# Peer expert retrieval in a two-layer trunk: the U dot products read the normed tokens from SBUF instead of from a copy in PSUM

## What is computed

```
def peer(h, wq, sub_keys, peer_u, peer_v):
    ...
    def block(xb):                       # 128 tokens
        ...                              # scores, three top-16, giving idx
        idx = jnp.take_along_axis(cidx, pos, axis=-1)      # (128, 8 heads, 16)
        g = jax.nn.softmax(sc, axis=-1)
        act = jax.nn.gelu(jnp.einsum('nd,nhkd->nhk', xb, peer_u[idx]), approximate=False)
        w = (g * act).astype(xb.dtype)
        return jnp.einsum('nhk,nhkd->nd', w, peer_v[idx])
```

## Time and profile before

| what | value |
| --- | --- |
| median of 3 runs | 4716.82 us (4715.45 to 4723.3) |
| the profiled execution's own time | 4724.11 us |
| its span, first to last instruction | 4722.3 us |
| PE busy | 3807.0 us, 81% |
| DVE busy | 2801.9 us, 59% |
| POOL busy | 2699.4 us, 57% |
| ACT busy | 1047.4 us, 22% |
| DMA packets of the POOL queue | 1342.34 MB of 1454.78 MB |

### The profile page before, as it was taken

The page is one execution under the profiler, slowest core; times in us unless marked ns, Lnnn a source line. Parts: engine busy times, 40 slices in busy tenths (PEclk is TensorE's granted clock), DMA queues, the critical chain, the costliest instruction groups (busy, mean ns, idle before and its releaser), DMA issues.

```text
span 4722.3 us, 40282 instructions
## 1 busy us (share of the span) xinstructions
PE 3807.0 (81%) x11914; PEld 1770.3 (37%) x11914; DVE 2801.9 (59%) x6305; ACT 1047.4 (22%) x2385; POOL 2699.4 (57%) x2759
## 2 busy tenths in 40 slices
PE   6999776888888888888778997688878878878877
PEld 3466532333333333333224575333333333333332
DVE  1612547666666667667634455576676776666763
ACT  1122211222222222222212141122222222222221
POOL 1800006667667667667755500277777777777775
PEclk8999588999999999999998995899999999999999
DMA  5112139999999999999981101399999999999998
GB/s 182 37 55 81 39 121 358 398 404 403 398 394 404 396 394 400 399 398 403 403 351 51 33 24 69 110 410 409 409 405 406 404 406 406 405 404 405 402 407 341
DMA packets 512186, 1454.78 MB, mean 308 GB/s; under 512 B 52896, under 2 KB 171108, under 8 KB 511844
## 3 DMA queue, kind: packets, MB, share of 16 engines
q0 software_dynamic: 368640, 1342.34, 72.0%
q1 hardware_dynamic: 143336, 109.91, 7.5%
HBM read 1448.83 MB, written 3.24 MB: 307 GB/s over the span
## 4 chain that ended last, share of the span: by engine, by line
DMA 30%; PE 27%; POOL 18%; DVE 15%; issue 8%; ACT 1%; DVEq 1%; SPq 0%; ACTq 0%; POOLq 0%
PE ps L536 26%; DMA arena<-in_peer_v,expert_rows 15%; DMA arena<-in_peer_u,expert_rows 14%; POOL arena L511 9%; POOL arena L519 9%; DVE arena L1351 5%; PE ps L640 1%; DVE arena L1268 1%; DVE arena L1299 1%; DVE top_indices L1298 0%; DVE arena L1330 0%; DVE arena L1333 0%; DVE chosen_pair L1335 0%; DVE top_values L1301 0%; DVE arena L1281 0%
## 5 line engine op out<-in xcount | busy, mean ns | idle before, releaser
L536 PE MATMUL ps<-arena 128*128 128x512 f32 (+7 forms) x9648 | 3456.3, 508 | 759.7 <-DMA arena<-in_peer_v,expert_rows 613.4
L536 PEld LDWEIGHTS ps<-arena 128*128 128x128 f32 (+3 forms) x9648 | 1553.4, 198 | 2628.3 <-DMA arena<-in_peer_v,expert_rows 1428.9
L1351 DVE CUSTOM_DVE_ANT_0 arena<-arena,ps 128x1024 f32<-128x1024 f32 x1280 | 1529.3, 1219 | 959.3 <-DMA arena<-in_peer_u,expert_rows 957.0
L511 POOL DMA_INDIRECT arena<-in_peer_u,expert_rows x1280 | 1220.2, 953 | 772.5 <-issue 307.9
L519 POOL DMA_INDIRECT arena<-in_peer_v,expert_rows x1280 | 1207.6, 943 | 416.2 <-issue 327.3
L1102 ACT ACTIVATE arena<-constants,expert_weight 128x128 f32<-128x128 f32 x1280 | 478.9, 396 | 1084.6 <-PE ps L536 1060.8
L498 POOL MEMSET arena<- 128x5632 f32 x2 | 9.6, 4792 | 414.1 <-ACTq L254 414.1
L1196 DVE TENSOR_REDUCE score_max<-ps 128x1 f32<-128x640 f32 (+1 forms) x80 | 57.4, 718 | 306.0 <-PE ps L536 306.0
L536 PE MATMUL ps<-arena,cond_silu 128*2 128x128 f32 (+1 forms) x1344 | 187.5, 294 | 18.6 <-DMA arena<-in_ada_w 10.7
L491 POOL TENSOR_SCALAR arena<-arena,vec_columns 128x512 f32<-128x512 f32 x120 | 151.9, 1276 | 10.2 <-issue 10.2
L536 PEld LDWEIGHTS ps<-arena,cond_silu 128*2 128x2 f32 x1344 | 109.4, 86 | 114.4 <-issue 76.8
(11 more groups left out here) (156 smaller groups left out, 1823.5 us busy)
## 6 DMA issues: line engine op xcount, KB each, us to landing
arena<-in_ada_w SPq DMA_DIRECT2D x80, 512.0 KB
arena<-in_peer_u,expert_rows POOLq DMA_INDIRECT x1280, 11.2
arena<-in_peer_v,expert_rows POOLq DMA_INDIRECT x1280, 11.3
arena<-in_w_in SPq DMA_DIRECT2D x32, 512.0 KB, 4.0
arena<-in_ada_w SPq DMA_DIRECT2D x4, 2048.0 KB, 15.9
arena<-in_w_out SPq DMA_DIRECT2D x4, 2048.0 KB, 7.9
arena<-in_peer_wq SPq DMA_DIRECT2D x2, 4096.0 KB, 18.2
peer_modulation<-modulation_rows SPq DMA_DIRECT2D x4, 1536.0 KB, 12.1
```

Of the source, the lines that this page charges most:

```text
L511: pool.indirect_dma_start(UR[:, k % RING, :], None, u_rows, bass.IndirectOffsetOnAxis(ap=rows[:, g % LIVE, k:k + 1], axis=0))\
L536: return pe.matmul(out, lhsT, rhs, start=start, stop=stop)
L1351: dve.tensor_tensor_reduce(out=UR[:, k % RING, :], in0=UR[:, k % RING, :], in1=pair(1), scale=1.0, scalar=0.0, op0=ALU.mult, op1=ALU.add, ...
```

## The change

The dot product takes H2 itself as its second operand, and the copy of H2 into PSUM goes, with one of the two drains (waits for DVE's own pipeline) around it.

```
                     dve.wait_ge(u_in[k % RING], n * 32 + 16 * (k // RING + 1))
-                    dve.tensor_tensor_reduce(out=UR[:, k % RING, :], in0=UR[:, k % RING, :], in1=pair(1),
+                    dve.tensor_tensor_reduce(out=UR[:, k % RING, :], in0=UR[:, k % RING, :], in1=H2[:, (g // HEADS) % 2, :],
                                              scale=1.0, scalar=0.0, op0=ALU.mult, op1=ALU.add,
                                              accum_out=act_h[:, k:k + 1]).then_inc(S["u_free"], 1)
...
                     if h == 0:
-
-                        dve.drain()
-                        dve.tensor_copy(pair(1), H2[:, t % 2, :])
                         dve.drain()
                     head_dots(l, g)
```

## The result

The changed kernel takes 4896.6 us (median of 4 runs, 4880.1 to 4904.5) where the kernel before takes 4716.1 beside it: a ratio of 1.038 with an interval of 1.036 to 1.039, about 180 us more.

The account below looks back on a forecast made before the run. Transfers were taken to bound the kernel, POOL 4% behind; held gathers would make POOL the bound. Layer 1 +138, layer 2 +226 and the copy -3 gave +361 us on 4717, stated as 5080 us; range 4950 to 5215.

Parts of the forecast that it names:

- What bounds the kernel: Peer half's loop of gathers: transfers set the pace at 1.299 us each, POOL's 1.246 us is second, 4% behind.
- The copy: Ten copies of H2 into PSUM go: 2.7 us off the path at layers' first tiles, bounds 0 to -13.5, taken -3.
- The hold: POOL's gather starting x into a two-SBUF-input DVE instruction of duration d loses d - x - 0.13, ending 0.81 us after it.
- The size per dot product: Isolated dot products, those that waited for their row: mean loss to POOL of 0.48 us each, at any phase alike.
- rival B: Landing time ties dot products to POOL's clock; steps take 42.2 us, about 4740 us in all; chance 0.06.
- The term for held gathers: POOL's loss in each step of 32 gathers: 6.5 us by today's mix, 7.7 with all isolated, taken 7.1.
- The bursts: Back-to-back dot products at pitch 1.14 us: two gathers take three dot products, 3.42 us for 2.49, losing 0.31 per dot product.
- The two kinds of dot product: Isolated and back-to-back dot products weighted 0.57 x 0.48 + 0.43 x 0.31 = 0.41 us, 6.5 us a step, raised to 7.1.
- The profile after: Gather lines: some 40% run 1.0 to 2.0 us, mean about 1.17, 2990 us busy, peer stretch about 355 GB/s.
- The sum: Whole kernel: layer 1 138 us longer, layer 2 226, copy -3, together +361 us.
- A: Nothing holds the gathers and the copies are saved: 4714 us, at best 4703; chance 0.08.
- C: A burst of about 8 dot products shuts POOL out: 51.2 us a step, +681, about 5400 us; chance 0.06.

Follow-up runs that it names:

- psum_no_copy: Kernel before, with the copy of H2 into PSUM made only once in a layer, at the first tile: 4715.0 us, ratio 0.9999.
- keep_copy: Kernel before, with only the operand changed: the copy is made but dot products read H2 in SBUF: 4897.0 us, ratio to before 1.039.
- the shifts: Changed kernel with a reduction over 128 or 320 columns of unused PSUM ahead of each dot product: 4783.6 and 4922.3 us.
- shift_tiny_late: Changed kernel with a reduction over 40 PSUM columns ahead of dot products k = 8 to 15 alone: 4727.3 us, ratio to before 1.0019.

## Why the prediction was right and where it was wrong

- **What bounds the kernel.** Right: the transfers, with POOL's 1.246 us a few per cent behind. After the change POOL's share of the chain, the shorter landing and the equal layers all say that POOL took over. POOL's slack in the sum was right too: 1905 less 284 leaves 146 us below layer 1's 1767 and 58 below layer 2's 1679, and POOL gave up 151 and 61 us of idle time.
- **The copy.** I counted -3 us. `psum_no_copy` and `keep_copy` cannot tell it from nothing.
- **The dot product on DVE.** Right: 1226 ns against 1220.
- **The hold.** Right, as read from the earlier trace rows: a gather that starts inside a two-input DVE instruction ends 0.81 us after it. The rule of the Trainium skill, "SBUF — State Buffer", "Who interferes with whom", that such an instruction contends with a GpSimd instruction that reads SBUF, holds for this custom instruction too; its inference that a tensor-tensor leaves DMAs alone does not hold for these indexed gathers, as the tensor-tensor of the earlier trace rows shows. The section says of DVE's 2-port modes that whoever issues first has the shared pair for the whole instruction and the other is blocked. The rows here agree in that a held gather waits for the dot product's end; they differ in who is first, since a gather that starts up to 0.04 us after a dot product is let in ahead of it.
- **The size per dot product: the step that failed.** I wrote that an isolated dot product's window catches one start of POOL "at any phase alike" and took the mean over a uniform phase, 0.48 us. Measured was 0.28, because 298 of 760 starts sit at the window's trailing edge and lose some 0.06. I had seen that phases could arrange themselves (rival B) but tied them to the landing time and gave it 0.06; the shifts refuted that form of it. What the rows suggest instead is that the slower of two periodic engines pushes the faster one. The term for held gathers, 7.1 us a step or 284 us a layer beside the 8 of before, came out as 4.9 a step or 196 beside them (393 in both layers). That is 88 of the 91 and 93 us by which the layers were forecast too long.
- **The bursts.** 0.31 was close to the 0.34 measured, in part by luck. I took a held gather's successor for free because it meets less than 0.13 us of the running dot product; the rows show that it starts 0.03 to 0.05 us into the one after, and is free only if that is under about 0.04.
- **The two kinds of dot product.** I weighted them by their number and even raised the isolated ones' share. Padding the later half alone, in `shift_tiny_late`, leaves 9 us of the 180: the bursts' holds fall from 179 to 44 us and the isolated ones' from 209 to 125. And a hold of either kind costs time only beyond POOL's slack in its layer.
- **The profile after.** I expected 40% of the gathers at 1.0 to 2.0 us, a mean of 1.17, 2990 us busy and 355 GB/s. It was 34%, 1.10, 2821 and 375, for the same reason.
- **The sum.** 138 + 226 was forecast, 48 + 133 measured. The direction was right; the size was twice what it should have been, because the fixed slack is taken from a loss that was itself too large: 284 less 58 against 194 less 61 in layer 2.
- **Rivals A and C.** A is refuted by the rows. C, that a burst shuts POOL out, is refuted by the burst above, in which a gather is let in at the end of each dot product it waits for.

What is not settled: the remaining isolated starts (462 of 760) are spread over the window, perhaps because a burst or a pause resets the phase, and no run took that apart. Which access of a gather is the one that waits was not tried.

## What to carry to other kernels

Before giving a DVE instruction its second SBUF input, look at what POOL does beside it: the copy into PSUM looked like waste, cost nothing that these runs can tell, and was what kept the gathers going. When two periodic engines exclude each other, don't price it by chance; write down both periods. Of the four pitches run here the one just short of a match (1.14 against 1.24 us) and the longest (1.55) cost most, and 0.1 us of padding gave nearly all of it back. Slack on the second bound is spent once and stage by stage, so compare the added busy time with the idle time of that engine in each stage.

## What was not expected of the hardware

A reduction of 40 PSUM columns ahead of each of 1280 dot products made the changed kernel 168 us faster (4729.0 against 4896.6). In the bursts shown POOL takes the dot products' period, at 1.25, 1.345 and 1.55 us, with holds of 0.01, 0.10 and 0.30 us in every gather. A DVE instruction with two SBUF inputs can itself wait about 0.07 us for a gather that starts up to 0.04 us after it (1.29 us long at 3826.08).
